# Narrower second block of an expert pass, a new order of the expert passes, and small edits around them

## What is computed

```python
logits = jnp.einsum('btd,de->bte', h, router_w) + router_b
top_val, top_idx = lax.top_k(logits, TOP_K)            # TOP_K = 2, N_EXPERTS = 8
top_w = jax.nn.softmax(top_val, axis=-1)
out += combine[..., e:e + 1] * _swiglu(h, w_gu[e], w_down[e])
# _swiglu: (silu(h @ gate) * (h @ up)) @ w_down,  gate, up: 1024 x 1792, w_down: 1792 x 1024
```

## Time and profile before

| | us |
|---|---|
| median of 3 runs | 1453.7 (1451.06 to 1455.21) |
| the profiled execution's own time | 1456.0 |
| its span, first to last instruction | 1454.4 |
| PE busy in the span | 1373.7 (94%) |
| DVE, ACT, POOL busy | 887.6, 725.8, 213.5 |
| mean granted clock of PE | 0.985 |

### The profile page before, as it was taken

One profiled execution on the slowest core, in us unless ns is written; L12 is line 12 of the kernel. 1 busy time (PEld: TensorE's weight loads), 2 busy tenths in 40 slices (PEclk: granted clock), 3 DMA queues, 4 the chain that ended last, 5 costly groups with the idle time before them and its releaser, 6 DMA issues.

```text
span 1454.4 us, 20841 instructions
## 1 busy us (share of the span) xinstructions
PE 1373.7 (94%) x6944; PEld 1129.6 (78%) x6944; DVE 887.6 (61%) x1184; ACT 725.8 (50%) x1123; POOL 213.5 (15%) x280
## 2 busy tenths in 40 slices
PE   6999889999999999998889899999999999999986
PEld 2766468999999879986567588888888888888874
DVE  1325557363333484224876697655555999999977
ACT  1323555322333353323434685445445888888863
POOL 1010000070000004103420644100000700000110
PEclk9999999999999999999989999999999999999998
DMA  9786673369443424446655699766656999999991
GB/s 349 227 306 226 217 231 113 116 238 330 131 127 122 129 58 133 116 173 222 235 196 176 235 381 352 253 191 217 206 180 184 369 369 366 371 367 371 370 371 61
DMA packets 254102, 341.24 MB, mean 235 GB/s; under 512 B 15886, under 2 KB 209708, under 8 KB 253900
## 3 DMA queue, kind: packets, MB, share of 16 engines
q1 hardware_dynamic: 241354, 299.55, 62.8%
q0 software_dynamic: 12432, 40.70, 7.5%
q10 hardware_dynamic: 242, 0.01, 0.0%
HBM read 318.13 MB, written 21.02 MB: 233 GB/s over the span
## 4 chain that ended last, share of the span: by engine, by line
PE 80%; DVE 8%; DMA 3%; ACT 3%; issue 3%; SPq 2%; POOL 0%; DVEq 0%; ACTq 0%
PE PS L2259 24%; PE PS L508 14%; PE PS L2266 11%; PE PS L484 7%; PE PS L485 7%; PE PS L486 7%; PE PS L630 2%; SPq L2040 1%; DMA BIG<-in_moe_w_gu 1%; PE PS L2231 1%; DMA BIG<-in_poolm 1%; PE PS L655 1%; DMA raw<-in_w_in_a 1%; ACT whi L2057 1%; DMA raw<-in_ada_w 1%
## 5 line engine op out<-in xcount | busy, mean ns | idle before, releaser
L460 DVE TENSOR_TENSOR wlo<-raw,whi 128x1024 fp32r<-128x1024 f32 x130 | 168.1, 1319 | 225.5 <-ACT whi L457 225.2
L2061 DVE TENSOR_TENSOR wlo<-BIG,whi 128x1024 fp32r<-128x1024 f32 x192 | 239.2, 1263 | 72.7 <-ACT whi L2057 69.7
L2057 ACT ACTIVATE whi<-BIG 128x1024 fp32r<-128x1024 f32 x192 | 202.5, 1059 | 70.6 <-PE PS L2259 37.6
L2259 PE MATMUL PS<-whi,Hh 128*128 128x512 f32 x560 | 223.1, 398 | 0.8 <-DVE Hl L2129 0.7
L2259 PE MATMUL PS<-whi,Hl 128*128 128x512 f32 x560 | 218.7, 391 | 0.0
L2259 PE MATMUL PS<-wlo,Hh 128*128 128x512 f32 x560 | 218.1, 389 | 0.0
L484 PE MATMUL PS<-Hh,whi 128*128 128x384 f32 (+1 forms) x624 | 208.8, 335 | 4.2 <-DVE Hl L794 2.2
L486 PE MATMUL PS<-Hh,wlo 128*128 128x384 f32 (+1 forms) x624 | 207.8, 333 | 0.0
L485 PE MATMUL PS<-Hl,whi 128*128 128x384 f32 (+1 forms) x624 | 207.6, 333 | 0.0
L2061 DVE TENSOR_TENSOR wlo<-raw,whi 128x1024 fp32r<-128x1024 f32 x144 | 177.4, 1243 | 46.3 <-ACT whi L2057 44.7
L2057 ACT ACTIVATE whi<-raw 128x1024 fp32r<-128x1024 f32 x144 | 152.2, 1059 | 55.7 <-PE PS L2266 30.2
(11 more groups left out here) (399 smaller groups left out, 1955.7 us busy)
## 6 DMA issues: line engine op xcount, KB each, us to landing
raw<-in_moe_w_gu SPq DMA_DIRECT2D x224, 256.0 KB, 6.8
BIG<-in_moe_w_gu SPq DMA_DIRECT2D x224, 256.0 KB, 6.5
raw<-in_ada_w SPq DMA_DIRECT2D x96, 512.0 KB, 5.1
BIG<-in_moe_w_down SPq DMA_DIRECT2D x80, 512.0 KB, 8.0
raw<-in_ffn_w_gu SPq DMA_DIRECT2D x44, 512.0 KB, 4.8
raw<-in_w_in_c SPq DMA_DIRECT2D x32, 512.0 KB, 4.0
raw<-in_moe_w_down SPq DMA_DIRECT2D x32, 512.0 KB, 8.0
scr_tok<-BIG POOLq DMA_DIRECT2D x28, 512.0 KB, 9.9
```

Of the source, the lines that this page charges most:

```text
L460: self.eng.tensor_tensor(wlo[:, s, :], raw[:, s, :], whi[:, s, :].bitcast(f32), ALU.subtract).then_inc(lo_made, 1)
L2057: act.activation(whi[:, slot(v), :], moe_raw(v), ACT.Copy).then_inc(hi_made, 1)
L2061: dve.tensor_tensor(wlo[:, slot(v), :], moe_raw(v), whi[:, slot(v), :].bitcast(f32), ALU.subtract).then_inc(lo_made, 1)
L2259: last = pe.matmul(PS[:, 6 * b + c % 2, :], lhs, wt[:, s, 512 * k:512 * k + 512], start=(q == 0 and k == 0 and lhs is h and wt is whi), st ...
```

## The change

It has five parts.

1. **Half block.** The second block of a twin pass has at most 64 tokens. Its stationary operand holds the upper parts of the 64 tokens in columns 0 to 63 and their lower parts in columns 64 to 127, so PSUM rows 0 to 63 get `h x w`, rows 64 to 127 `l x w`. PE issues the `whi` and `wlo` matmuls only (the lower part by `wlo` is added too). The halves are summed before SiLU and at the pass's end.
2. **Which passes.** An expert of 1 to 6 with 129 to 192 tokens gets a twin pass (128 + 64); one with 193 to 256 gets two single passes. Expert 7's first block is always the last pass.
3. **Order.** Pass 0, then the single passes, then the twin passes, then the last one. `pool_pick` now runs between single and twin passes; its buffer `pick_n` moves to `ht`.
4. **mLSTM edges.** The last unit of the v projection signals each token tile by itself, so that the copies of tiles 0 and 1 run beside it; PE waits for one copy ahead of the scores, for all ahead of the transpose; the first exponentials and their table load move ahead of the copies. At the end of the mLSTM the first split of the output projection comes one unit earlier.
5. **Fillers.** `keep_clock` of 4, 5 and 8 matmuls (384 columns, bank 1) between the router's logits, and of 6 in `pe_route`.

```diff
@@ pe: n_last, stage 2
                 pe_logits_sum(pe, 0)
                 pe_logits_sum(pe, 1)
+                keep_clock(pe, 4, 1)
                 pe_logits(pe, 2)
                 pe_hn(pe, 2, (0,))
+                keep_clock(pe, 5, 1)
                 pe_logits_sum(pe, 2)
                 pe_hn(pe, 2, (1,))
+                keep_clock(pe, 8, 1)
@@ pe_mixer1
-            for k in range(KT):
-                n_product(pe, U_INC_N + k, Hh[:, k, :], Hl[:, k, :], k == 0, k == KT - 1)
+            for k in range(KT - 1):
+                n_product(pe, U_INC_N + k, Hh[:, k, :], Hl[:, k, :], k == 0, False)
+            n, k = U_ADA_LATE - 1, KT - 1
+            pe.wait_ge(lo_made, split_count(n))
+            n_tile(pe, n, 0, Hh[:, k, :], Hl[:, k, :], False, True).then_inc(gates_mm, 1)
+            n_tile(pe, n, 1, Hh[:, k, :], Hl[:, k, :], False, True).then_inc(gates_mm, 1)
+            n_tile(pe, n, 2, Hh[:, k, :], Hl[:, k, :], False, True).then_inc(unit_used, 1)
...
-                            pe.wait_ge(v1_act, TT)
-                            pe.wait_ge(v1_dve, TT)
+                            pe.wait_ge(v1_act, 1)
+                            pe.wait_ge(v1_dve, 1)
@@ act_mixer1 (the same line in dve_mixer1, after the product with num of unit NM - 2)
+                    if u == NM - 2:
+                        sp_.upto(U_OUTC)
@@ pe_route
             pe.wait_ge(hn_copied, 6)
+            keep_clock(pe, 6, 4)
             pe.wait_ge(route_step, 5)
@@ pool_table
-            pool.tensor_copy(dbl[:, 1:NE], over[:, 1:NE])
+            pool.tensor_scalar(over3, count, 192.0, None, ALU.is_gt)
...
+            ch.step(pool.tensor_tensor(dbl[:, 1:NE - 1], over[:, 1:NE - 1], over3[:, 1:NE - 1], ALU.subtract))
...
-            ch.step(pool.tensor_scalar(cap, dbl, 256.0, None, ALU.mult))
+            pool.tensor_scalar(cap, dbl, 192.0, None, ALU.mult)
@@ act_pass
                 if kind == "gu" and q == 3:
-                    for b in blocks_:
-                        act.activation(gp[:, b, c % 2, :], PS[:, 6 * b + c % 2, 0:256], ACT.Silu
-                                       ).then_inc(esilu_made[b], 1)
+                    act.activation(gp[:, 0, c % 2, :], PS[:, c % 2, 0:256], ACT.Silu).then_inc(esilu_made[0], 1)
+                    if twin:
+                        act.activation(half_gu, PS[0:64, 6 + c % 2, :], ACT.Copy).then_inc(esilu_made[1], 1)
...
                     act_unit_hi(act, w + RING, p)
+                if twin and kind == "gu" and q == 3:
+                    act.wait_ge(eprod_made[1], at[1] * 2 * MC + (2 * c + 1))
+                    act.activation(half_gu[:, 0:256], half_gu[:, 0:256], ACT.Silu).then_inc(esilu_made[1], 1)
@@ dve_pass
+                    if twin:
+                        dve.wait_ge(esilu_made[1], at[1] * (2 * MC + 1) + (2 * c + 1))
+                        dve.tensor_tensor(half_gu, half_gu, PS[64:128, 6 + c % 2, :], ALU.add).then_inc(eprod_made[1], 1)
...
                     dve_unit_lo(dve, w + RING, p)
+                if twin and kind == "gu" and q == 3:
+                    dve.wait_ge(esilu_made[1], at[1] * (2 * MC + 1) + (2 * c + 2))
+                    dve.tensor_tensor(half_gu[:, 0:256], half_gu[:, 0:256], half_gu[:, 256:512],
+                                      ALU.mult).then_inc(eprod_made[1], 1)
...
+            if twin:
+                dve.wait_ge(esilu_made[1], at[1] * (2 * MC + 1) + (2 * MC + 1))
+                dve.tensor_tensor(half_y, half_y, PS[64:128, 4:6, :], ALU.add).then_inc(y_made[1], 1)
@@ pe_pass
-                            for lhs, wt in ((h, whi), (h, wlo), (l, whi)):
+                            parts = ((h, whi), (h, wlo), (l, whi)) if b == 0 else ((h, whi), (h, wlo))
+                            for i, (lhs, wt) in enumerate(parts):
@@ pe_experts (act, dve and pool alike)
-            pe_pass(pe, 0, False, (0, 1))
-            n2, n = passes(pe)
-            with pe.Fori(1, n2 + 1) as p:
-                pe_pass(pe, p, True, (0, 1))
-            with pe.Fori(n2 + 1, n) as p:
-                pe_pass(pe, p, False, (0,), n2)
-            pe_pass(pe, n, False, (), n2, final=True)
+            pe_pass(pe, 0, 0, False, (0, 1))
+            first, twins = passes(pe)
+            with pe.Fori(1, first) as p:
+                pe_pass(pe, p, 0, False, (0,))
+            with pe.Fori(1, twins + 1) as q:
+                pe_pass(pe, q + first - 1, q, True, (0, 1))
+            pe_pass(pe, first + twins, 0, False, (), twins, final=True)
```

More of the change, by code:

```diff
@@ L1530, in dve_rows, with act_decay @@
             dve.tensor_scalar(gm[:, 1:2], gm[:, 0:1], -1.0, None, ALU.mult).then_inc(rows_made, 1)
+        def act_decay(act, u):
+            h, d, r = unit(u)
+            act.wait_ge(row_in[u // 8], 80)
+            if u >= 2:
+                act.wait_ge(num_made, u - 1)
+            for key in range(3):
+                last = act.activation(key_blocks(E[:, u % 2, :], d, key), key_rows(neg_rows[:, T * u:T * u + T], d, key),
+                                      ACT.Exp, bias=nat[:, key, r:r + 1])
+            last.then_inc(e_made, 1)
         def act_mixer1(act, ch, sp_):
@@ new lines, in pool_table @@
+            ch.step(pool.tensor_scalar(over, count, 128.0, None, ALU.is_gt))
+            pool.tensor_tensor(sgl, over, over2, ALU.add)
+            ch.step(pool.tensor_tensor(dbl[:, 1:NE - 1], over[:, 1:NE - 1], over3[:, 1:NE - 1], ALU.subtract))
+            prefix(cd, dbl)
+            pool.tensor_scalar(cap, dbl, -2.0, None, ALU.mult)
+            ch.step(pool.tensor_scalar(sgl[:, 1:NE - 1], sgl[:, 1:NE - 1], 1.0, None, ALU.add))
+            ch.step(pool.tensor_tensor(sgl, sgl, cap, ALU.add))
@@ L1934, in pool_table @@
-            ch.step(pool.tensor_tensor(far, far, over[:, 7:8].to_broadcast([128, NE]), ALU.add))
             ch.step(pool.tensor_tensor(far, far, cap, ALU.subtract))
@@ L1972, in pool_pick @@
         def pool_pick(pool, ch):
-            over, over2, cd, cs = (bb[:, i, :] for i in (0, 1, 4, 5))
-            ch.step(pool.tensor_scalar(over, cd, 256.0, -FAR, ALU.mult, ALU.add))
-            ch.step(pool.tensor_scalar(over2, cs, 128.0, None, ALU.mult))
-            ch.step(pool.tensor_tensor(over, over, over2, ALU.add))
+            over, near = bb[:, 0, :], bb[:, 7, :]
+            ch.step(pool.tensor_scalar(over, near, -FAR, None, ALU.add))
             for kk in range(2):
@@ L2033, in sp_experts @@
                     sp.dma_start(dst, src).then_inc(moe_full[v % MRING], 16)
-            n2, n = passes(sp)
-            with sp.Fori(0, n) as j:
+            first, twins = passes(sp)
+            with sp.Fori(0, first + twins) as j:
                 e = sp.value_load(ctl[0:1, bass.ds(j + 2, 1)], min_val=0, max_val=NE - 1)
@@ L2144, in dve_pass @@
+            first, twins = passes(act)
+            with act.Fori(1, first) as p:
+                act_pass(act, p, 0, False, (0,))
+            with act.Fori(1, twins + 1) as q:
+                act_pass(act, q + first - 1, q, True, (0, 1))
+            act_pass(act, first + twins, 0, False, (), last=True)
+        def dve_pass(dve, p, q_, twin, nxt, last=False, ch=None):
             blocks_ = range(2 if twin else 1)
+            at = turns(p, q_)
             def product_lo(c):
                 for b in blocks_:
-                    dve.wait_ge(eguh_made[b], (p - b) * MC + (c + 1))
@@ L2332, in pool_experts @@
             pool_counts(pool, ch)
-            n2, n = passes(pool)
+            first, twins = passes(pool)
             pool.wait_ge(scattered, 96)
```

227 lines of the change are left out of this document (123 added, 104 removed).

## The result

The changed kernel takes 1444.32 us (median of 5 runs, 1442.12 to 1446.89), the kernel before 1453.21 us in the same measurement. The ratio is 0.9943, 95% interval 0.9925 to 0.9961: faster, by 8.9 us instead of the 22.3 forecast, and 1.3 us above the upper end of the range. The profiled execution took 1446.22 us, with a span of 1444.6.

What follows compares the result with a forecast made beforehand. PE was taken to set the pace in every pass, with no load bandwidth left in single ones. -17.6 - 7.0 + 1.5 + 7 - 1.8 - 2.3 - 2.1 = -22.3 us gave a median of 1431.4, range 1420 to 1443.

Steps and rivals of the forecast that it cites:

- Steps 5 to 7: mLSTM start, mLSTM end and router: earlier sums, earlier split and clock fillers, -6.2 us together.
- Step 4: Single passes in a row: late loads and POOL slowing DVE's splits use up slack, +7 us, bounds 0 and 15.
- (b): Pass 1: DVE's splits slow beside POOL's six norm operations, 10 us behind less a 4.9 reserve: 5 us.
- (a): Six single passes and the norm's weights shrink a 20.2 us load lead; loads due 11.5 us ahead, PE loses 6.7.
- rival B: Expert passes: single passes in a row cost 15 us, or the half block's chain loses its cover: 1439 to 1443; chance 0.18.
- step 4 costs nothing, by the bytes: Single passes in a row: 22 MB at 370 GB/s take 59.5 us, under 60.8, so no loss: 1424; chance 0.15.
- Rival C: Boundaries of passes 2 to 7: load stalls recur at 7 us each, slower from four events on, six give 1466; chance 0.05.
- Steps 1 and 3: Expert passes: one twin plus two singles replace two twins, -17.6 us; half block's new chain delays PE in last chunk, +1.5.
- Step 2: Last pass: a twin pass ahead of it restores the load lead, so its stall goes, -7.0 us.
- Steps 5 and 6: mLSTM: sums start earlier with V copies beside the projection, -1.8 us; output projection's first split comes earlier, -2.3.
- Step 7: Router: clock fillers in PE's waits keep the full clock, -2.1 us.
- three signs that I had named for a wrong forecast: A single pass over 63 us beyond pass 1, a twin pass over 103 us, or not nine passes.

Runs made afterwards that it cites:

- lighter-load kernel: Changed kernel loading only the left half of each down weight in every pass but the first, norm in its place: 1442.93 us, ratio 0.9927.
- norm-late kernel: Changed kernel with POOL's six norm operations and next norm load moved behind the single passes: 1444.04 us, ratio 0.9929.
- table of four kernels: Changed kernel with norm beside single or twin passes, each with full or lighter loads: 1444.3 and 1444.0 us full, 1442.9 and 1433.1 us lighter.

## Why the prediction was right in sign and wrong in size

**Direction and structure: right.** The time fell, by 8.9 us and not 22.3. Nine passes, the 204-token expert as two singles, the 187-token one twin, no stall in the last pass. Steps 5 to 7 are a gain of the forecast's order.

**Step 4: the step that failed.** It was +7 and is +13, the largest part of the miss, and both of its terms were mis-sized. As far as the rows show, one assumption is behind both: that the six units of split weights ahead of PE are a reserve. They hold weights only. The product's two parts are made by the same ACT and DVE queues, behind the split of a unit six further on; when that split is late, for whatever reason, PE stops with full buffers.
- In (b) I took 10 us behind less a reserve of 4.9 (from 7.2 us of PE work, which is five units at 1.45 and not six). The reserve is not there: the lighter-load kernel has the whole delay (stops of 1.2 and 8.6) and 2 us of half clock behind it, 12.8 us. Nor was (b) nothing, as I had given for a DVE without gaps: from 893 on DVE had none, and POOL's operations still ran between its splits.
- In (a) I let a load be due 11.5 us ahead of its pass. It is due 17.4 ahead. Of the 20.2 us of lead only 2.8 could be used, not 8.7. With 17.4 in its place my own sum gives 12.6 us instead of 6.7, and the kernel without POOL's operations measured 13.3; less the 2.8 for the norm's weights it gives 9.8, and the norm-late kernel measured 10.6. The loss per single pass was near (1.8 us against 2.1 from the earlier trace rows). How the 5.9 us between 11.5 and 17.4 arise is not worked out unit by unit.
- That the two don't add, because loads catch up while PE stands, was right, and the table of four kernels shows it. The upper bound of 15 did contain the value, and rival B (1439 to 1443) came nearest to the time.

The rival "step 4 costs nothing, by the bytes" left 1.05 MB of token store and fetch out: 22.0 MB alone would be 59.7 us, under PE's 60.7; with them a pass needs 62.5. Rival C's count was off too: four events (28 - 7 = 21 us) would only have used up the 22.3 us of gain.

**Steps 1 and 3.** The twin pass takes 103.9 us against 100.4 + 1.5. The stop of 1.28 us in its last chunk is there as worked out. Of the other 2 us the trace shows 1.5 in the product's transposes, which I had made cheaper: the 28 of them (L2294, L2297) take 4.1 us of PE's time from start to start, against 2.6 for the 28 of a twin pass before (L2231). Why they are slower is open.

**Step 2**: -6.6 against -7.0, right. It is a gain of the order of passes: with the twin pass first the last pass is at 67.7 again.

**Steps 5 and 6**: 2.5 us (4.73 less the router's 2.25) against 4.1. The output projection begins earlier but its second tile waits 1.65 us for DVE's product, and at the start the sums run 1.0 us earlier instead of 1.8. **Step 7**: -2.25 in the profile against -2.1, right there, though not in each execution.

**What the order of the passes was worth.** The change puts the twin pass last but one and so saves 6.6 us in the last pass, but it takes away the twin pass that stood behind pass 0, where it hid POOL's norm at a cost of 3.7 us and filled the buffers ahead of the singles. Undoing the order alone makes the six singles 12.6 us shorter, the twin pass 3.7 and the last pass 6.9 longer in the profiles, 2.3 us net in the expert stage; the medians say 4.7.

Of the three signs that I had named for a wrong forecast, one came, a twin pass over 103 us, and it was not the one that mattered. That was pass 1, which the bound of 63 us left out.

## What to carry to other kernels

A ring of prepared operands is slack only if nothing else that the consumer needs is made behind it in the same in-order queue. Before counting a buffer's depth as reserve, ask what stands behind the instruction that fills it. When two causes each delay the same chain, test them two by two: taking away either one here gave at most 1.4 us, within the ranges of the runs, and both gave 11 us (with part of the loads left out, so this is a test and not a version to use).

## What the runs showed of the hardware

- DVE and POOL took turns, instruction by instruction. Beside a 128x1024 operation of POOL (3.3 us) DVE finished exactly one instruction with both inputs in `SBUF`, even when DVE had the next one ready at once: three splits in 9.96 us. A product with an input in `PSUM` kept its 0.41 us between them (896.38). A 64x256 product of DVE beside POOL in the norm-late kernel took 2.57 us as well. The Trainium skill ("SBUF — State Buffer", "Who interferes with whom") calls this an exclusive lock that the instruction issued first holds to its end. The trace agrees, with the loss on both sides: POOL's operations take 3.2 to 3.4 us there, the first one 2.42.
- At a DMA share of 1.07 to 1.08 the rate stood at 365 to 371 GB/s, mostly 369 or 370, in the single passes of the kernels with full loads, whether a pass took 60.7 or 62.5 us. So the bytes of a pass (23.08 MB) over a rate taken from another kernel gave the length of a pass without lead to 0.1 us.
- The same instruction in unchanged code starts up to 5 us apart between profiles of kernels that are identical up to there (452.3 to 457.3). Stages are better compared from a common instruction than from the span's start.
